# A hybrid encoder layer: TensorE's projection matmuls moved ahead of the turn in each attention unit

## The chip, the cores and the metric

The kernel runs on one core of a Trainium2 chip. The metric is device time in microseconds (us), the median of several runs. TensorE (PE in the profile, with its weight loads as PEld) does the matmuls and transposes, VectorE is DVE, ScalarE is ACT, GpSimd is POOL, and SyncE (SP) starts most DMAs.

## The reference

One layer on 1024 tokens of 1024 features: a half-step feed-forward block, a mixing block, a second half-step feed-forward block, each with a modulated layer norm ahead and a layer norm behind. The change lies in the mixing block:

```python
def _mixer(u, w_in, rpb, w_out):
    proj = u @ w_in                      # [qA kA vA | qB kB vB]
    ...
    ya = _dilated_attention(heads_a(qa), heads_a(ka), heads_a(va))
    yb = _neighbourhood_attention(heads_b(qb), heads_b(kb), heads_b(vb), rpb)
    return jnp.concatenate([ya, yb], axis=-1) @ w_out
```

Group A has 8 heads of 64 features with dilated windows, group B 8 heads with a two-dimensional neighbourhood of keys and a learned bias. Each is a softmax of masked scores times values.

## The kernel before, in words

The program runs phase after phase: modulation, feed-forward 1, a boundary phase, attention A, attention B, output projection, feed-forward 2. `attention_phase` is called twice, as phase A (tiles named `a_...`) and phase B (`b_...`).

A phase handles four pairs of heads. A pair has 16 units (`NU`): 8 blocks of 128 queries times 2 heads. So a phase has 64 units (`U`), and TensorE's program is one loop over s = 0 to 67. What a unit needs of each engine is handed on by semaphores:

- `score(s)`: TensorE computes the scores of unit s. In A that is a 128x256 product (L2082) and four 32-row products of 256 columns (L2085); in B one product of 128x384 (L2091). The program's fp32 matmul shows as two in the trace (so L2082 x2, L2085 x8, L2091 x2).
- `step(s)` on VectorE: waits for the scores, takes the reciprocal of unit s-2's row sums (L1962), adds the bias and takes the row minimum (L1967), then scales the exponentials of unit s-2 into `pn` (L1974).
- `exponential(s)` on ScalarE (L1876), behind L1967.
- `turn(s - LAG)`, with `LAG = 3`: TensorE transposes the 128x512 (A, four pieces) or 128x384 (B, three pieces) of `pn` (L2101) into a PSUM bank of `a_tr` or `b_tr`. It waits for `pn` of unit s-3, which VectorE makes in `step(s - 1)`, and for its bank.
- `turned_out` on ScalarE: copies that bank to SBUF (L1884). It stands in ScalarE's program behind `exponential(s)`, and ahead of the copies of projection results (`take`) and of the rounding of the next weights (`split`, L1869).
- `project(p + 1, ...)`: in each unit of pairs 0 to 2, TensorE runs `SPREAD = 9` of the 144 matmuls (L2042, 128x512, fp32r) which give the next pair's keys, queries and values. Pair 3 has no next pair, so its 16 units have no projection.
- Every eighth unit from s = 11 on ends with `multiply` (L2127, weights times values).
- Five units of a pair in A and four in B (unit 4 of pairs 1 to 3 on) end with `values(p, g)`: three or four transposes of values (L2069) into a bank of the same two banks, which VectorE copies out (L1922).

Each of TensorE's steps starts with waits of its own, and the engine takes its instructions in the program's order. VectorE's copy L1922 of group g stands in its program behind `step`, `take` and `split` (L1914, which waits for ScalarE's L1869).

Of the kernel before, what the change touches and what calls it, by code (L numbers as in the profile page):

```python
# [31 lines left out]
HP = HEADS // 2  # L32
# [1562 lines left out]
def band_start(t):  # L1595

    return min(max(P * t - HD, 0), S - BAND)
# [43 lines left out]
def attention_phase(nc, top, tag, w_in, w_at, w_next, y_at, ut_hi, ut_lo, scratch, ident, bias_in, tab, y_t,  # L1641
# [21 lines left out]
    SPREAD = 9  # L1663
# [12 lines left out]
    def outputs(p):  # L1676

        return [(j, half) for j in ((2, 1, 0) if p == 0 else (1, 0, 2)) for half in range(HALVES)]

    def output_at(p, j, half):  # L1680
        return NPJ * p + outputs(p).index((j, half))
# [9 lines left out]
    def split_at(g, j):  # L1691

        return 3 * (g - 1) + ((2, 1, 0) if g == 1 else (1, 0, 2)).index(j) + 1

    def values_due(s):

        p, g = s // NU, s % NU - LAG - 1
        return (p, g) if 1 <= p < HP and 0 <= g < NVG else None

    def half_due(s):  # L1700

        h = (s - LAG) // UN - 1
        return h if s >= LAG and (s - LAG) % UN == 0 and 0 <= h < 2 * HP else None
# [16 lines left out]
    with ExitStack() as st:  # L1720
# [302 lines left out]
        def _(pe):  # L2023
            def wait_taken(n):
                pe.wait_ge(pj_v, taken(n, True))
                if taken(n, False):
                    pe.wait_ge(pj_s, taken(n, False))

            def project(p, first, last):

                for x in range(first, last):
                    i, y_ = x // FULL, x % FULL
                    j, half = outputs(p)[i]
                    n = NPJ * p + i
                    if y_ == 0:
                        if p >= 1:
                            pe.wait_ge(w_lo, split_at(p, j))
                        if n >= 2:
                            wait_taken(n - 2)
                    k, m = y_ // 3, y_ % 3  # L2040
                    l, r = ((wh, ut_hi), (wh, ut_lo), (wl, ut_hi))[m]
                    done = nc.tensor.matmul(pj[:, half, :], l[:, k, j, :], r[:, k, NB * half:NB * half + NB],  # L2042
                                            start=y_ == 0, stop=y_ == FULL - 1, skip_group_check=True)
                    if y_ == FULL - 1:
                        done.then_inc(pj_mm, 1)
# [17 lines left out]
            def values(p, g):  # L2063
                if g == 0:
                    wait_taken(output_at(p, 2, 1))
                bank_free(("v", p, g))
                for x in range(VB * g, min(VB * g + VB, NV)):
                    at = P * (x - VB * g)
                    last = nc.tensor.transpose(tr[:, turn_at["v", p, g] % 2, at:at + P], value_source(x), ident[:, :])  # L2069
                last.then_inc(v_tr, 1)  # L2070

            def score(u):
                p, m, b = u // NU, u % NU, u % 2
                t, i = m // 2, m % 2
                if m == 0:
                    wait_taken(output_at(p, 0, 1))
                if u >= 2:
                    pe.wait_ge(low, u - 1)
                own = q[:, p % 2, i, :]
                if dil:  # L2080
                    w0 = band_start(t)
                    nc.tensor.matmul(sc[:, b, 0:BAND], own[:, P * t:P * t + P], keys[:, p % 2, w0:w0 + BAND],  # L2082
                                     start=True, stop=True, skip_group_check=True)
                    for r in range(CL):
                        last = nc.tensor.matmul(sc[CQ * r:CQ * r + CQ, b, BAND:BAND + CK],  # L2085
                                                own[:, P * t + CQ * r:P * t + CQ * r + CQ], kc[:, p % 2, r, :],
                                                start=True, stop=True, skip_group_check=True)
                else:
                    cb, rb = t // RBS, t % RBS
                    grid = keys[:, p % 2, :].rearrange("p (r c) -> p r c", c=COLS)  # L2090
                    last = nc.tensor.matmul(sc[:, b, 0:W], own[:, P * t:P * t + P],  # L2091
                                            grid[:, 4 * rb:4 * rb + KR, KC0[cb]:KC0[cb] + KC],
                                            start=True, stop=True)
                last.then_inc(qk, 1)

            def turn(u):
                b = u % 2
                pe.wait_ge(divided, u + 1)
                bank_free(("t", u))
                for c in range(NC):  # L2100
                    last = nc.tensor.transpose(tr[:, turn_at["t", u] % 2, P * c:P * c + P], pn[:, b, P * c:P * c + P],  # L2101
                                               ident[:, :])
                last.then_inc(p_tr, 1)

            def multiply(h):
                p, half = h // HALVES, h % HALVES
                pe.wait_ge(p_out, UN * (h + 1))
                if half == 0:
                    pe.wait_ge(v_out, NVG * (p + 1))
                if p >= 1:  # L2110
                    pe.wait_ge(y_out, HALVES * (p - 1) + half + 1)
                todo = products(dil, half)
                for n, (x, users, cls) in enumerate(todo):
                    for i in range(2):
                        to = o[HD * i:HD * i + HD, half, :]
                        if cls is not None:
                            to = to.rearrange("p (t r m) -> p t r m", r=CL, m=CQ)[:, :, cls]
                            of = pt[:, i, :, users[0][1], CQ * cls:CQ * cls + CQ]
                        else:
                            t, ch = users[0]  # L2120
                            to = to[:, P * t:P * (t + len(users))]
                            of = pt[:, i, t, ch]
                            if len(users) == 2:
                                at, step = (t * NC + ch) * P, (NC - 1) * P
                                of = pt_flat[:, i, at:at + 2 * step].rearrange(
                                    "p (a s) -> p a s", s=step)[:, :, 0:P]
                        last = nc.tensor.matmul(to, vt[:, x, HD * i:HD * i + HD], of, start=(n == 0),  # L2127
                                                stop=(n == len(todo) - 1), skip_group_check=True)
                last.then_inc(pv, 1)
# [8 lines left out]
            for s in range(U + LAG + 1):  # L2138
                p, m = s // NU, s % NU
                if s < U:  # L2140
                    score(s)
                if LAG <= s < U + LAG:
                    turn(s - LAG)
                if p + 1 < HP:
                    project(p + 1, SPREAD * m, SPREAD * m + SPREAD)
                if half_due(s) is not None:
                    multiply(half_due(s))
                if values_due(s):
                    values(*values_due(s))
# [213 lines left out]
```

## Time and profile before

| | before |
|---|---|
| median of 3 runs | 2155.69 us (2155.47 to 2156.41) |
| profiled execution | 2155.39 us, of which the span is 2153.5 us |
| PE / PEld / DVE / ACT / POOL busy | 91% / 71% / 56% / 37% / 32% |
| phase A, units 3 to 47 (turn and projection) | 858.5 to 1048.4 us |
| phase B, units 3 to 47 | 1152.15 to 1308.1 us |

The busy shares are averages over the whole layer. The stretches in the last two rows are the ones in which a unit has both a turn and projection matmuls. The time per unit is read there as the distance between the starts of two scores.

### The profile page before, as it was taken

The numbers are of one execution on the slowest core, as the hardware profiler recorded it, in microseconds if no ns is written. First come the engines' busy times: TensorE is split into PE (matmuls) and PEld (weight loads), VectorE is DVE, ScalarE is ACT, GpSimd is POOL, SyncE is SP. The second block draws the span as 40 slices with busy tenths as digits, with TensorE's granted clock in tenths as the row PEclk, the third lists the DMA queues.
The fourth block names the chain that finished last, engine by engine and source line by source line (L and its number), as shares of the span: only waits on it lengthen the run. The fifth ranks groups of instructions, "written<-read, shape, count | busy, mean of one in ns | idle before, by whom it ended". The sixth has DMA issues, their size and how long they took to land. (4 is left out here: it accounts for less than half of the span.)

```text
span 2153.5 us, 27570 instructions
## 1 busy us (share of the span) xinstructions
PE 1970.2 (91%) x10086; PEld 1536.9 (71%) x10086; DVE 1205.6 (56%) x2047; ACT 792.2 (37%) x1367; POOL 696.5 (32%) x488
## 2 busy tenths in 40 slices
PE   3999999999999938999889998894999999999996
PEld 2777777777878726677567775673888888888884
DVE  4865555545687973344423445467744444457778
ACT  2623333332434242433423344315433333334441
POOL 0653334332960020000023222232734343339400
PEclk6999999999999969999999999897999999999998
DMA  6255545454874133011032220603233332357732
GB/s 255 93 159 179 166 148 184 153 168 149 317 246 151 45 108 97 21 49 49 11 81 59 49 59 11 223 22 117 93 103 118 98 105 92 102 191 287 259 108 98
DMA packets 184663, 270.58 MB, mean 126 GB/s; under 512 B 12353, under 2 KB 110929, under 8 KB 184401
## 3 DMA queue, kind: packets, MB, share of 16 engines
q1 hardware_dynamic: 153410, 234.45, 32.3%
q10 hardware_dynamic: 30096, 30.25, 4.5%
q0 software_dynamic: 1024, 4.13, 1.2%
q8 instruction: 81, 1.33, 0.3%
q14 instruction: 52, 0.43, 0.1%
HBM read 210.85 MB, written 57.93 MB: 125 GB/s over the span
## 5 line engine op out<-in xcount | busy, mean ns | idle before, releaser
L1474 PE MATMUL f_ps<-f_uh,f_ops 128*128 128x512 f32 x2496 | 787.2, 392 | 5.9 <-DVE f_ops L1232 4.2
L1474 PEld LDWEIGHTS f_ps<-f_uh,f_ops 128*128 128x128 f32 x2496 | 468.7, 188 | 128.1 <-issue 25.3
L1474 PE MATMUL f_ps<-f_ul,f_ops 128*128 128x512 f32 x1248 | 486.0, 389 | 0.0
L1474 PEld LDWEIGHTS f_ps<-f_ul,f_ops 128*128 128x128 f32 x1248 | 234.5, 188 | 46.8
L1333 DVE TENSOR_TENSOR f_dl<-f_blocks,f_dh 128x1024 fp32r<-128x1024 f32 (+1 forms) x146 | 200.1, 1384 | 86.3 <-ACT f_dh L1158 86.0
L1158 ACT CAST f_dh<-f_blocks 128x1024 fp32r<-128x1024 f32 (+1 forms) x146 | 144.4, 990 | 229.0 <-PE f_ps L1581 222.9
L1581 PE MATMUL f_ps<-f_dh 128*128 128x512 f32 x496 | 195.9, 395 | 9.9 <-DVE f_ev L1367 5.3
L1232 DVE TENSOR_TENSOR f_ops<-f_sums,f_ops 128x512 fp32r<-128x512 f32 x160 | 122.4, 765 | 142.9 <-ACT f_ops L1045 142.9
L984 POOL TENSOR_TENSOR f_sums<-f_raw 128x512 f32<-128x512 f32 x80 | 107.4, 1342 | 280.2 <-DVE f_ops L1232 210.3
L1581 PE MATMUL f_ps<-f_dl,f_dh 128*128 128x512 f32 x496 | 194.9, 393 | 0.0
L1581 PE MATMUL f_ps<-f_dh,f_dl 128*128 128x512 f32 x496 | 194.8, 393 | 0.0
L1232 DVE TENSOR_TENSOR f_ops<-f_raw,f_ops 128x512 fp32r<-128x512 f32 x136 | 107.0, 789 | 112.3 <-ACT f_ops L1045 112.2
L2042 PE MATMUL in_pj<-ut_hi,in_wh 128*128 128x512 f32 x376 | 158.8, 422 | 9.2 <-PEq L2327 4.7
L1272 DVE TENSOR_TENSOR acc<-acc,f_ps 128x512 f32<-128x512 f32 x120 | 82.5, 687 | 139.2 <-PE f_ps L1474 139.0
L2042 PE MATMUL in_pj<-ut_hi,in_wl 128*128 128x512 f32 x376 | 149.3, 397 | 0.0
L2042 PE MATMUL in_pj<-ut_lo,in_wh 128*128 128x512 f32 x376 | 148.1, 394 | 0.0
L1581 PEld LDWEIGHTS f_ps<-f_dh 128*128 128x128 f32 x496 | 94.2, 190 | 33.8 <-DVE f_dl L1333 14.5
L1045 ACT CAST f_ops<-f_sums 128x512 fp32r<-128x512 f32 x160 | 95.5, 618 | 37.7 <-PE f_ps L1474 16.4
L1581 PEld LDWEIGHTS f_ps<-f_dh,f_dl 128*128 128x128 f32 x496 | 94.3, 190 | 19.9
L1581 PEld LDWEIGHTS f_ps<-f_dl,f_dh 128*128 128x128 f32 x496 | 94.1, 190 | 19.2
L1834 POOL MEMSET b_q<- 64x1024 f32 x4 | 3.7, 945 | 287.6 <-POOLq L2327 287.5
L1860 POOL TENSOR_TENSOR b_bias<-b_runs,b_mask 128x384 f32<-128x384 f32 x48 | 49.2, 1057 | 134.9 <-DVE b_sm L1967 112.5
(233 smaller groups left out, 3146.0 us busy)
## 6 DMA issues: line engine op xcount, KB each, us to landing
f_hidden<-acc SPq DMA_DIRECT2D x154, 256.0 KB, 3.8
f_blocks<-f_hidden SPq DMA_DIRECT2D x154, 256.0 KB, 3.4
f_blocks<-in_ffn_w_down SPq DMA_DIRECT2D x132, 256.0 KB, 5.8
f_raw<-in_ffn_w_gate SPq DMA_DIRECT2D x22, 1024.0 KB, 6.2
f_raw<-in_ffn_w_up SPq DMA_DIRECT2D x22, 1024.0 KB, 5.4
f_aw<-in_w_ada ACTq DMA_DIRECT2D x28, 512.0 KB, 3.5
acc<-in_w_ada ACTq DMA_DIRECT2D x28, 512.0 KB, 3.7
in_raw<-in_w_in SPq DMA_DIRECT2D x24, 512.0 KB, 4.0
```

What stands on the lines that cost most here:

```text
L984: nc.gpsimd.tensor_tensor(sums[:, x], of, with_, how).then_inc(s_done, 1)
L1045: nc.scalar.copy(op(o)[0], source(o)).then_inc(w_hi, 1)
L1158: nc.scalar.copy(high_of(n), operands(n)).then_inc(d_hi, 1)
L1232: nc.vector.tensor_tensor(op(o)[1], source(o), op(o)[0].bitcast(F32), ALU.subtract).then_inc(w_lo, 1)
L1272: nc.vector.tensor_tensor(to, t_in, ps[:, bank, :], ALU.add).then_inc(done, 1)
L1333: nc.vector.tensor_tensor(low_of(n), operands(n), high_of(n).bitcast(F32), ALU.subtract).then_inc(d_lo, 1)
L1474: done = nc.tensor.matmul(ps[:, bank, :], l[:, k, :], r[:, k, :], start=fresh and k == 0 and m == 0, stop=closed and k == HK - 1 and m == ...
L1581: done = nc.tensor.matmul(ps[:, bank(r, t), :], left[m][:, x, P * t:P * t + P], right[m], start=r in OPENS and k == 0 and m == 0, stop=r i ...
L1834: nc.gpsimd.memset(q[HD * (1 - i):HD * (2 - i), par, i, :], 0.0).then_inc(zeroed, 1)
L1860: nc.gpsimd.tensor_tensor(b, run, m, ALU.add).then_inc(b_ready, 1)
L2042: done = nc.tensor.matmul(pj[:, half, :], l[:, k, j, :], r[:, k, NB * half:NB * half + NB], start=y_ == 0, stop=y_ == FULL - 1, skip_group ...
```

## The change

In TensorE's loop, `project` now stands directly behind `score`, and `turn` behind `project`. Nothing is added or removed, no other engine's program differs, and no DMA is moved.

```diff
                 if s < U:
                     score(s)
+                if p + 1 < HP:
+                    project(p + 1, SPREAD * m, SPREAD * m + SPREAD)
                 if LAG <= s < U + LAG:
                     turn(s - LAG)
-                if p + 1 < HP:
-                    project(p + 1, SPREAD * m, SPREAD * m + SPREAD)
                 if half_due(s) is not None:
                     multiply(half_due(s))
                 if values_due(s):
```

On TensorE's queue in phase A this is one unit of pair 0, with a turn and neither `multiply` nor `values`. `a_sc` is the scores' PSUM tile, `in_pj` the projection's, and a row of the order is one matmul of the program.

```order
 L2082 MATMUL a_sc<-a_k,a_q 128x256
 L2085 MATMUL a_sc<-a_kc,a_q 32x256 x4
+L2042 MATMUL in_pj<-ut_hi,in_wh 128x512
+L2042 MATMUL in_pj<-ut_lo,in_wh 128x512
+L2042 MATMUL in_pj<-ut_hi,in_wl 128x512
...
 L2101 MATMUL a_tr<-ident,a_pn 128x128 x4
-L2042 MATMUL in_pj<-ut_hi,in_wh 128x512
-L2042 MATMUL in_pj<-ut_lo,in_wh 128x512
-L2042 MATMUL in_pj<-ut_hi,in_wl 128x512
...
```

The four transposes L2101 stood between the scores and the nine projection matmuls, and now stand between the ninth of these and the next unit's scores.

On TensorE's queue in phase A these are the rows around a unit that also has a group of value transposes (`a_tr<-ident,a_v`).

```order
+L2042 MATMUL in_pj<-ut_hi,in_wl 128x512
 L2101 MATMUL a_tr<-ident,a_pn 128x128 x4
-L2042 MATMUL in_pj<-ut_hi,in_wh 128x512
-L2042 MATMUL in_pj<-ut_lo,in_wh 128x512
-L2042 MATMUL in_pj<-ut_hi,in_wl 128x512
...
 L2069 MATMUL a_tr<-ident,a_v 128x128 x4
 L2082 MATMUL a_sc<-a_k,a_q 128x256
 L2085 MATMUL a_sc<-a_kc,a_q 32x256 x4
```

Here the turn now stands directly ahead of the value transposes, where nine matmuls lay between them; both still stand behind this unit's scores and ahead of the next unit's.

## Rows read from the trace of the kernel before

**Rows 1.** The page: span of the profiled execution.

```profile
span 2153.5 us, 27570 instructions
```

**Rows 2.** Busy time by stretch: start:end, length, PE, PEld, DVE, ACT, POOL, PEclk, DMA, GB/s.

```profile
858.50:1048.40 189.90, 189.17 (x1355) 133.40 (x1355) 81.14 (x218) 74.60 (x158) 0.00 (x0) 1.00 0.12 36
1048.40:1098.00 49.60, 39.37 (x382) 24.17 (x382) 25.32 (x76) 23.68 (x54) 0.00 (x0) 1.00 0.03 12
1152.15:1308.10 155.95, 155.54 (x824) 118.41 (x823) 68.50 (x235) 62.42 (x158) 41.88 (x50) 1.00 0.20 45
```

**Rows 3.** Waits of PE, 858.5 to 1048.4: total us, times, longest.

```profile
PE a_tr L2069 <- DVE acc L1922: 0.7, 2, 0.4
```

**Rows 4.** Waits of PE, 1152.1 to 1308.1.

```profile
PE b_tr L2069 <- DVE acc L1922: 0.4, 1, 0.4
```

**Rows 5.** Timeline, PE, phase A: two units without a turn, then one.

```profile
852.01 0.59 PE L2082 MATMUL a_sc<-a_k,a_q 128*128 128x256 f32 x2
...
853.10 0.50 PE L2042 MATMUL in_pj<-ut_hi,in_wh 128*128 128x512 f32 x1
...
858.54 0.59 PE L2082 MATMUL a_sc<-a_k,a_q 128*128 128x256 f32 x2
...
859.64 0.66 PE L2101 MATMUL a_tr<-ident,a_pn 128*128 128x128 f32 x4
```

**Rows 6.** Timeline, PE, phase A: scores five units apart, with turns.

```profile
902.71 0.59 PE L2082 MATMUL a_sc<-a_k,a_q 128*128 128x256 f32 x2
...
921.04 0.59 PE L2082 MATMUL a_sc<-a_k,a_q 128*128 128x256 f32 x2
```

**Rows 7.** Timeline, PE, phase A: value transposes behind projection, first and fourth group.

```profile
931.98 0.39 PE L2042 MATMUL in_pj<-ut_hi,in_wl 128*128 128x512 f32 x1
932.21 0.60 PE L2069 MATMUL a_tr<-ident,a_v 128*128 128x128 f32 x4
932.65 0.60 PE L2082 MATMUL a_sc<-a_k,a_q 128*128 128x256 f32 x2
...
944.30 0.39 PE L2042 MATMUL in_pj<-ut_hi,in_wl 128*128 128x512 f32 x1
945.05 0.75 PE L2069 MATMUL a_tr<-ident,a_v 128*128 128x128 f32 x4 [0.37 <-DVE acc L1922]
```

**Rows 8.** Timeline, PE, last pair of A: a turn between two scores.

```profile
1052.67 0.66 PE L2101 MATMUL a_tr<-ident,a_pn 128*128 128x128 f32 x4
1053.17 0.60 PE L2082 MATMUL a_sc<-a_k,a_q 128*128 128x256 f32 x2
```

**Rows 9.** Timeline, PE, phase B: scores around two units without and three with turns.

```profile
1146.70 0.81 PE L2091 MATMUL b_sc<-b_k,b_q 128*128 128x384 f32 x2
...
1152.15 0.81 PE L2091 MATMUL b_sc<-b_k,b_q 128*128 128x384 f32 x2
...
1161.27 0.81 PE L2091 MATMUL b_sc<-b_k,b_q 128*128 128x384 f32 x2
```

**Rows 10.** Timeline, PE, phase B: scores of one later unit and the next.

```profile
1200.78 0.81 PE L2091 MATMUL b_sc<-b_k,b_q 128*128 128x384 f32 x2
...
1203.83 0.81 PE L2091 MATMUL b_sc<-b_k,b_q 128*128 128x384 f32 x2
```

**Rows 11.** Timeline, all engines, phase A: around the fourth group of value transposes.

```profile
939.97 0.56 ACT L1884 COPY acc<-a_tr 128x512 f32<-128x512 f32 x1
...
940.42 0.61 PE L2069 MATMUL a_tr<-ident,a_v 128*128 128x128 f32 x4
...
941.38 1.06 ACT L1869 CAST in_wh<-in_raw 128x1024 fp32r<-128x1024 f32 x1
...
943.17 1.22 DVE L1914 TENSOR_TENSOR in_wl<-in_raw,in_wh 128x1024 fp32r<-128x1024 f32 x1
```

**Rows 12.** Timeline, PEld, phase A: weight loads of a turn and of value transposes.

```profile
900.13 0.42 PEld L2101 LDWEIGHTS a_tr<-ident,a_pn 128*128 128x128 f32 x4 [0.41 <-issue]
...
931.99 0.59 PEld L2069 LDWEIGHTS a_tr<-ident,a_v 128*128 128x128 f32 x4
```

## The prediction

> **What bounds the kernel now.** I first looked at the busy time by stretch, to see whose time a unit takes. In phase A, from unit 3 to unit 47, TensorE is busy for 189.17 of 189.90 us, VectorE for 81, ScalarE for 75; in phase B it is busy for 155.54 of 155.95 us [rows 2]. So in the units where the order changes, TensorE sets the time, at its full granted clock (1.00), and nobody else comes near. The last pair of A is another matter: no projection, TensorE busy for 39.37 of 49.60 us [rows 2]. There the order of instructions stays as it was.
>
> Then the waits of TensorE in these stretches: 0.7 us in A over two places and 0.4 us in B at one [rows 3, 4], all of them value transposes waiting for VectorE's copy out of their bank. The turn never waits here. That is the number that matters most: the obvious hope of the change is that projection work covers a turn that waits for `pn`. There is no such wait to cover. The turn of unit s-3 needs `pn` from `step(s - 1)`, which needs only the scores of the unit before; at its old place it was in time, and at its new place it comes a whole projection later.
>
> So all that is left is what TensorE itself pays for the changed neighbours, and what the later turn does to ScalarE. I read the first from starts in the timeline, since the busy durations overlap.
>
> **The change, part by part.**
>
> *A unit of A without a turn* is scores, then nine projection matmuls, then the next scores. This is just what the changed unit begins with. Two such units take 858.54 - 852.01 = 6.53 us, 3.265 each [rows 5]. The adjacency scores to projection is therefore measured in this trace.
>
> *A unit of A with a turn, old order*: (921.04 - 902.71)/5 = 3.666 us [rows 6]. The turn between scores and projection costs 3.666 - 3.265 = 0.401 us.
>
> *The turn at its new place*, behind projection and ahead of scores. The nearest row is the group of four value transposes, which stands exactly there, with the same shape and number: it starts 0.23 us after the last projection matmul (as any next matmul does) and the scores start 932.65 - 932.21 = 0.44 us later [rows 7]. So the new unit is 3.265 + 0.44 = 3.705 us, 0.04 more than before. The far row on one side is a turn between two scores in the last pair: 1053.17 - 1052.67 = 0.50 us [rows 8], 0.10 more than now. On the other side I see no reason why the turn should cost less than its present 0.40, so zero. I take the value transposes, since they have the same left and right neighbour; the last pair's turn has scores on its left.
>
> Why the difference? The trace shows the turn's first weight load starting only with its first matmul, 0.41 us after PEld's previous work, while the value transposes' first load, at 931.99, precedes its matmul at 932.21 [rows 7, 12]. Behind the scores somebody has to make that start uncovered: now the turn, afterwards the first projection matmul, which the 3.265 already contains. The Trainium skill, "TensorE: Matmul & The Clock Gate", section "Architectural detail: the array is 16x 32x32, not 1x 128x128", says that TensorE can pull weight loads ahead of matmuls in flight. Taken alone that speaks against any effect: loads hide at either place and the sum is 0. The rows agree with it behind projection and not behind A's 32-row scores.
>
> *How many.* 45 units in A (s = 3 to 47). In two of them the value transposes wait for VectorE: their start comes 945.05 - 944.30 = 0.75 us behind the last projection matmul, where 0.23 is normal [rows 7]. VectorE's time there counts from the scores, so 0.04 us vanish in that wait of 0.52. The five units that end with `multiply`, and those with value transposes, I count like the rest. 43 x 0.038 = 1.6 us.
>
> *Phase B.* Unit without a turn: (1152.15 - 1146.70)/2 = 2.725 us; with a turn (1161.27 - 1152.15)/3 = 3.04 [rows 9], and 1203.83 - 1200.78 = 3.05 further on [rows 10]. Three transposes behind projection are three quarters of 0.44, 0.33 us. New unit 3.055, so 0.005 to 0.015 more; 0.01 x 44 = 0.4 us. The gap is smaller since B's scores are full 128-row products.
>
> *ScalarE.* It takes its program in order, and the copy L1884 behind the turn now comes one projection later: that delays everything behind it (copies of projection results, the rounding L1869 of the next weights), and VectorE's L1914 waits for L1869, ahead of the very copy for which the value transposes wait. At that place, in the old order, the copy ran at 939.97 and L1869 at 941.38, with VectorE starting L1914 at 943.17 [rows 11]. In the new order the turn's transposes end where the value transposes begin now, 940.42 plus 0.04; its result is out some 0.2 us after, so the copy starts near 940.7, 0.7 us late. L1869 then runs from 942.1 and ends near 943.15. VectorE wants it at 943.17. The cover is used to the last hundredth; I take +0.1 us for the three places together (two in A, one in B), and up to 0.7 at each, 2.1 us, as the upper end. Elsewhere ScalarE is idle for over half of the stretch (75 of 190 us [rows 2]) and projection results are needed more than a unit after they are taken. The last pair starts with one copy pending, which fits ahead of its first exponential; I take 0. VectorE, GpSimd, SyncE and their DMAs keep their order, and no transfer is near its deadline here (DMA share 0.12 and 0.20 [rows 2]).
>
> **Sum.** 1.6 + 0.4 + 0.1 = +2.1 us. The span of 2153.5 us [rows 1] becomes 2155.6, the profiled execution's 2155.39 us 2157.5. That execution lies 0.3 us under the median of 2155.69, so a median would be near 2157.8; I give 2157.7. This is 0.1% slower, under the 0.2% (4.3 us) that a measurement of this kernel tells from no change.
>
> **The rivals.**
> - *The place makes no difference* (chance 0.20): the turn costs its 0.40 us anywhere, as by the pull-ahead of weight loads. For it: the B rows already differ by no more than their own spread, 3.04 against 3.05. Against: 0.44 read at the new place, in A. 2155.7 us.
> - *Slower: the turn pays its full price at the new place* (0.10). It has a wait for `pn` and one for its bank; if these keep its weight loads back even behind projection, it costs what it costs in the last pair, 0.50 us in A (+0.098 x 43 = 4.2 us), and in B the same 0.06 over three transposes, 0.39 (3.115 against 3.045: 0.07 x 44 = 3.1). Total +7.3: 2163.0 us. It counts as slower once a unit takes 0.05 us more on average. Against: value transposes also wait on semaphores there, and show 0.44.
> - *ScalarE hands the weights over late* (0.10): the three value waits grow by 0.7 each, 2.1 us in place of 0.1: 2159.8 us. For it: the missing slack above. Against: the arithmetic says just in time.
> - *Faster* (0.05): the three value waits go, 3 x 0.52 = 1.6 us, and the turn is not dearer: 2154.1 us. I see no mechanism, since VectorE's copy is not any earlier.
>
> My forecast itself, +1.2 to +2.8 us, has 0.55.
>
> **How the numbers follow.** The range leaves out the second and fourth rival and takes in the others with the spread of a median: 2154.9 to 2160.8 us. Faster by over 0.2% would need more than all waits of TensorE in both stretches: 0.03. Slower by over 0.2%: the second rival and a little of the third, 0.13. Within 0.2%: 0.84.
>
> **What would show it.** In the new trace: scores 3.70 to 3.71 us apart in plain units of A, 3.05 to 3.06 in B; from the turn's start to the next scores 0.44 in A and 0.33 in B; the first weight load of a turn ahead of its matmul; the copy L1884 at the start of the next unit; the three value waits at 0.5 to 0.6 us; the last pair of A still some 49.6 us. The prediction is wrong if turns start to wait for `pn` or a bank, if projection waits for its weights or its bank, or if the last pair changes by more than 1 us because ScalarE enters it late.

## The result and the profile after

The changed kernel takes 2159.24 us (median of 20 runs) where the kernel before takes 2155.83 us (median of 20 runs beside them). The ratio is 1.0017, 95% interval 1.0010 to 1.0024: 3.4 us slower by the medians, between 2.2 and 5.2 by the interval. The profiled execution took 2158.84 us, with a span of 2157.0 us.

The same two stretches, unit 3 to unit 47 of each phase, read as busy time by stretch (columns as in [rows 2]):

```profile
856.78:1048.65 191.87, 191.24 (x1354) 134.59 (x1353) 81.26 (x218) 77.79 (x157) 0.00 (x0) 1.00 0.11 36
1152.93:1308.94 156.01, 155.60 (x823) 119.52 (x822) 68.19 (x235) 65.41 (x157) 41.74 (x50) 1.00 0.19 45
```

Before, the same distances between scores were 1048.40 - 858.54 = 189.86 us in phase A and 1308.10 - 1152.15 = 155.95 us in phase B [rows 2, 5, 9]. So A grew by 2.0 us and B by 0.1 us. TensorE idles for 0.6 us in the stretch of A, where it idled for 0.7: the loss is no stall. It is in the distances of starts. The PE timeline of a plain unit of A:

```profile
897.72 0.60 PE L2082 MATMUL a_sc<-a_k,a_q 128*128 128x256 f32 x2
898.24 0.64 PE L2085 MATMUL a_sc<-a_kc,a_q 128*32 128x256 f32 x8
898.81 0.50 PE L2042 MATMUL in_pj<-ut_hi,in_wh 128*128 128x512 f32 x1
899.15 0.39 PE L2042 MATMUL in_pj<-ut_lo,in_wh 128*128 128x512 f32 x1
...
900.99 0.60 PE L2101 MATMUL a_tr<-ident,a_pn 128*128 128x128 f32 x4
901.43 0.60 PE L2082 MATMUL a_sc<-a_k,a_q 128*128 128x256 f32 x2
```

Read the first column. The turn now takes 901.43 - 900.99 = 0.44 us. The first projection matmul, behind the 32-row products, takes 899.15 - 898.81 = 0.34 us to the next start, where 0.23 is usual between projection matmuls. The unit takes 3.71 us against 3.666 [rows 6].

The turn's weights are now loaded ahead, starting 0.22 us before the matmuls (PEld timeline of the changed kernel; compare [rows 12]):

```profile
900.77 0.59 PEld L2101 LDWEIGHTS a_tr<-ident,a_pn 128*128 128x128 f32 x4
```

TensorE's waits in the stretch of A, against [rows 3]:

```profile
PE a_tr L2069 <- DVE acc L1922: 0.6, 2, 0.3
```

No turn waits, as none did before. In B it is one wait of 0.4 us, as in [rows 4]. And the place where ScalarE's delay could have hurt, all engines, against [rows 11]:

```profile
939.73 0.59 ACT L1884 COPY acc<-a_tr 128x512 f32<-128x512 f32 x1 [0.61 <-PE a_tr L2101]
...
939.98 0.60 PE L2082 MATMUL a_sc<-a_k,a_q 128*128 128x256 f32 x2
...
941.17 1.07 ACT L1869 CAST in_wh<-in_raw 128x1024 fp32r<-128x1024 f32 x1
...
942.28 1.22 DVE L1914 TENSOR_TENSOR in_wl<-in_raw,in_wh 128x1024 fp32r<-128x1024 f32 x1
```

ScalarE's rounding L1869 ends at 942.24 and VectorE's L1914 starts at 942.28, directly behind its own L1974. Before, L1869 ended at 942.44, 0.73 us ahead of L1914 [rows 11]. The later copy used up all this slack and cost nothing.

### The profile page after: what moved, and what is told of

Same layout as the page of the kernel before. It is cut to its first block and busy times, and to the rows that moved or that the text cites. A ratio compares the mean times of both kernels' runs of the same rounds, so it can differ in the third digit from the quotient of the medians.

```text
span 2157.0 us, 27570 instructions
## 1 busy us (share of the span) xinstructions
PE 1973.9 (92%) x10086; PEld 1540.4 (71%) x10086; DVE 1210.4 (56%) x2047; ACT 799.5 (37%) x1367; POOL 694.8 (32%) x488
## 5 line engine op out<-in xcount | busy, mean ns | idle before, releaser
L1333 DVE TENSOR_TENSOR f_dl<-f_blocks,f_dh 128x1024 fp32r<-128x1024 f32 (+1 forms) x146 | 204.7, 1413 | 83.7 <-ACT f_dh L1158 83.4
L2042 PE MATMUL in_pj<-ut_hi,in_wh 128*128 128x512 f32 x376 | 169.2, 450 | 9.2 <-PEq L2327 4.8
L2042 PEld LDWEIGHTS in_pj<-ut_hi,in_wh 128*128 128x128 f32 x376 | 71.8, 191 | 47.7 <-issue 29.4
```

Of the source, the lines that this page charges most:

```text
L1333: nc.vector.tensor_tensor(low_of(n), operands(n), high_of(n).bitcast(F32), ALU.subtract).then_inc(d_lo, 1)
```

## The experiments

Ratios are to the kernel before, run on the same chip. Their intervals are some 0.1% wide on either side (2 us), too wide to tell 2 us from 1 or 3. The stretches are far sharper. So each row gives both, and the verdict on a mechanism rests on the stretch. The stretches run from the scores of unit 3 to those of unit 48.

| kernel | ratio (95% interval) | A, us | B, us |
|---|---|---|---|
| before, again (e0_control) | 1.0001 (0.9992 to 1.0010) | 189.86 | 155.94 |
| changed | 1.0017 (1.0010 to 1.0024) | 191.87 | 156.01 |
| changed, again (e12_after_again) | 1.0018 (1.0010 to 1.0027) | 191.91 | 156.05 |
| A alone (e1_a_only) | 1.0010 (1.0001 to 1.0019) | 191.88 | 155.93 |
| B alone (e2_b_only) | 0.9994 (0.9985 to 1.0003) | 189.90 | 155.95 |
| turn behind the first projection matmul (e3_after_first) | 1.0016 (1.0007 to 1.0025) | 191.80 | 156.26 |
| one transpose in front, the rest behind (e4_split_turn) | 0.9995 (0.9986 to 1.0004) | 190.02 | 156.16 |
| 128-row scores last, old order (e8_wide_last_old) | 1.0012 (1.0003 to 1.0021) | 191.47 | 155.94 |
| 128-row scores last, new order (e9_wide_last_new) | 1.0016 (1.0007 to 1.0025) | 191.36 | 155.95 |
| values copied out first, old order (e7_values_first) | 0.9989 (0.9981 to 0.9998) | 188.45 | 155.29 |
| values copied out first, new order (e11_values_first_new) | 0.9994 (0.9986 to 1.0003) | 190.54 | 155.43 |
| LAG = 2, old order (e5_lag2_old) | 1.0698 (1.0680 to 1.0715) | 249.18 | 212.57 |
| LAG = 2, new order (e6_lag2_new) | 1.0143 (1.0128 to 1.0158) | 191.81 | 155.56 |

### The control, and each phase by itself

The control is the kernel before with no edit.

> The kernel before once more, unchanged, as a control. Of the 3.4 us measured for the change, the trace shows 2.0 us in the stretch with turn and projection of phase A and 0.1 us in that of phase B; the other 1.3 us lie in the other phases. Theory O (order alone, the rest is the spread of the other phases): ratio 1.000 within 0.001, and the phases before and behind attention differ from those of the first trace by 1 us or more all the same. Theory E (the change also lengthens other phases): the other phases of this run agree with the first trace within some tenths.

The stretches come back within 0.02 us. The rest of the span doesn't quite: 2153.8 - 189.86 - 155.94 = 1808.0 us in the control, and 2157.0 - 191.87 - 156.01 = 1809.1 us in the changed kernel. That is a difference of 1.1 us between different kernels; the control and the first profile of before agree to 0.3 us there, which leans to theory E. The repeat of the changed kernel, below, decides about it.

For one phase alone, the loop has `turn` on both sides of `project`, each with a condition:

```diff
-                if LAG <= s < U + LAG:
+                if LAG <= s < U + LAG and not dil:
                     turn(s - LAG)
                 if p + 1 < HP:
                     project(p + 1, SPREAD * m, SPREAD * m + SPREAD)
+                if LAG <= s < U + LAG and dil:
+                    turn(s - LAG)
```

That is A alone; B alone has the two conditions exchanged.

> The turn moved behind the projection in phase A alone. Theory O: the stretch from unit 3 to 47 of A is 2.0 us longer (191.9 in place of 189.9), B as before; time +2.0 us. Rival E: A alone gives only part of it, some +1.5 us, since B or the phases behind contribute the rest.

> The turn moved behind the projection in phase B alone. Theory O: the stretch of B changes by 0.1 us (0 to +0.4), time within 0.5 us of before. Rival E: +1 us or more although the stretch of B has not become longer.

A alone lengthens its stretch by 2.0 us and shows +0.10%, 2.2 us. B alone leaves its stretch as it was, and its interval reaches only to +0.03%. So the loss is phase A's, and B contributes nothing to speak of.

How far the whole time of A alone goes back to its stretch is less sure, for the profile shows a second thing. From the scores of unit 48 to those of unit 63, in the last pair of A, the changed kernel and A alone run the same instructions in the same order. Busy time there, first in the changed kernel, then in A alone (the eighth number is the mean granted clock):

```profile
1048.65:1091.70 43.05, 35.02 (x344) 21.32 (x342) 22.29 (x66) 19.22 (x43) 0.00 (x0) 1.00 0.03 13
1048.20:1092.59 44.39, 36.34 (x343) 22.29 (x342) 22.30 (x66) 19.20 (x43) 0.00 (x0) 0.96 0.03 13
```

In this pair TensorE is idle for 8 us, and in A alone its granted clock was 0.50 (1.2 GHz) from 1056.5 to 1059.9 us: the pair took 1.3 us longer. The profiles of e3, e7, e8, e9 and e11 show the same mean of 0.96 in this pair; both profiles of before, both of the changed kernel, B alone, e4, e5 and e6 show 1.00. Each of these other kernels was profiled once, so whether all their executions have the drop isn't shown. It lies outside the two stretches, but their ratios may contain it.

### What the neighbours cost

The turn is put behind the first of the nine projection matmuls, in both phases.

```diff
                 if p + 1 < HP:
-                    project(p + 1, SPREAD * m, SPREAD * m + SPREAD)
+                    project(p + 1, SPREAD * m, SPREAD * m + 1)
+                if LAG <= s < U + LAG:
+                    turn(s - LAG)
+                if p + 1 < HP:
+                    project(p + 1, SPREAD * m + 1, SPREAD * m + SPREAD)
```

> Both phases: the turn stands behind the first projection matmul of the unit, eight follow. Theory L (whatever stands behind A's four 32-row score products starts with an uncovered weight load, and the projection matmul pays 0.11 us for that start where the turn pays 0.06): a plain unit of A takes 3.71 us as in the changed kernel, time +2 us. Rival R (the turn costs more ahead of the next scores): a unit of A takes 3.67 us as before, time +0.

The PE timeline of one unit of A:

```profile
862.81 0.64 PE L2085 MATMUL a_sc<-a_kc,a_q 128*32 128x256 f32 x8
863.38 0.50 PE L2042 MATMUL in_pj<-ut_hi,in_wh 128*128 128x512 f32 x1
863.72 0.60 PE L2101 MATMUL a_tr<-ident,a_pn 128*128 128x128 f32 x4
864.07 0.48 PE L2042 MATMUL in_pj<-ut_lo,in_wh 128*128 128x512 f32 x1
864.39 0.39 PE L2042 MATMUL in_pj<-ut_hi,in_wl 128*128 128x512 f32 x1
```

The turn is nowhere near the next scores, and the stretch is 191.80 us all the same. Rival R (the turn costs more ahead of the next scores) gave 3.67 us a unit and the old stretch here, and falls. What this order shares with the changed one is the projection matmul directly behind the 32-row products, with its 0.34 us.

The 0.32 us behind the turn here (864.39 - 864.07) is not a second such price. Behind a turn the first projection matmul's recorded start comes early, and its distance to the next is longer by as much. So the turn has to be read up to the second projection matmul behind it: 864.39 - 863.72 = 0.67 us here, just four transposes at 0.11 and one matmul at 0.23. In the kernel before, where the turn stands behind the 32-row products, the same distance is 942.69 - 941.96 = 0.73 us, 0.06 more (PE timeline):

```profile
941.96 0.66 PE L2101 MATMUL a_tr<-ident,a_pn 128*128 128x128 f32 x4
942.37 0.47 PE L2042 MATMUL in_pj<-ut_hi,in_wh 128*128 128x512 f32 x1
942.69 0.39 PE L2042 MATMUL in_pj<-ut_lo,in_wh 128*128 128x512 f32 x1
```

The complement: one transpose stays behind the scores, the others go behind the projection (`pieces` says which of the turn's transposes are issued; the waits stay with the first, the signal with the last).

```diff
                 if LAG <= s < U + LAG:
-                    turn(s - LAG)
+                    turn(s - LAG, [0])
                 if p + 1 < HP:
                     project(p + 1, SPREAD * m, SPREAD * m + SPREAD)
+                if LAG <= s < U + LAG:
+                    turn(s - LAG, range(1, NC))
```

> Both phases: the first transpose of the turn stays directly behind the scores, the other three (two in B) stand behind the ninth projection matmul. Theory L: the first transpose takes the uncovered start, so a plain unit of A takes 3.67 us as before although three quarters of the turn are at the new place; time within 0.5 us of before. Rival R: three quarters of the loss, 3.70 us a unit, +1.5 us.

```profile
862.10 0.60 PE L2082 MATMUL a_sc<-a_k,a_q 128*128 128x256 f32 x2
862.62 0.64 PE L2085 MATMUL a_sc<-a_kc,a_q 128*32 128x256 f32 x8
863.19 0.33 PE L2102 MATMUL a_tr<-ident,a_pn 128*128 128x128 f32 x1
863.28 0.48 PE L2042 MATMUL in_pj<-ut_hi,in_wh 128*128 128x512 f32 x1
...
865.44 0.49 PE L2102 MATMUL a_tr<-ident,a_pn 128*128 128x128 f32 x3
865.77 0.60 PE L2082 MATMUL a_sc<-a_k,a_q 128*128 128x256 f32 x2
```

3.67 us a unit (865.77 - 862.10). Three of four transposes stand at the new place, and all but 0.2 of the 2.0 us is gone. So what matters in A is which instruction follows the 32-row products.

Last, the neighbour itself is changed: in A's scores the 32-row products come first and the 128-row product last (the signal moves to the last), with either order of turn and projection.

```diff
-                    nc.tensor.matmul(sc[:, b, 0:BAND], own[:, P * t:P * t + P], keys[:, p % 2, w0:w0 + BAND],
-                                     start=True, stop=True, skip_group_check=True)
                     for r in range(CL):
-                        last = nc.tensor.matmul(sc[CQ * r:CQ * r + CQ, b, BAND:BAND + CK],
+                        nc.tensor.matmul(sc[CQ * r:CQ * r + CQ, b, BAND:BAND + CK],
...
+                    last = nc.tensor.matmul(sc[:, b, 0:BAND], own[:, P * t:P * t + P], keys[:, p % 2, w0:w0 + BAND],
+                                            start=True, stop=True, skip_group_check=True)
```

> Order of before, but in A's scores the four 32-row products come first and the 128-row product last, so that the turn follows a 128-row product. Theory L: the turn's start is covered, its first interval 0.109 in place of 0.166 us, 0.06 us less per unit, 64 units: -3 to -4 us at most, less what the projection-to-32-row change costs (0 to 0.09 us per unit, which would eat it). Rival R: nothing changes but that cost.

> The changed kernel with the 128-row product last in A's scores. Theory L: now the first projection matmul is covered too, so the difference between the two orders goes: a plain unit of A takes the same as in the kernel with this edit and the old order, within 0.01 us. Rival R: the new order still costs 0.04 us per unit more.

In the old order:

```profile
863.12 0.40 PE L2042 MATMUL in_pj<-ut_hi,in_wl 128*128 128x512 f32 x1
863.44 0.64 PE L2083 MATMUL a_sc<-a_kc,a_q 128*32 128x256 f32 x8
864.01 0.70 PE L2086 MATMUL a_sc<-a_k,a_q 128*128 128x256 f32 x2
864.55 0.60 PE L2101 MATMUL a_tr<-ident,a_pn 128*128 128x128 f32 x4
864.90 0.47 PE L2042 MATMUL in_pj<-ut_hi,in_wh 128*128 128x512 f32 x1
865.22 0.39 PE L2042 MATMUL in_pj<-ut_lo,in_wh 128*128 128x512 f32 x1
```

The turn, read up to the second projection matmul, now takes 0.67 us in place of 0.73, since its start is covered; but the way into the 32-row products costs 0.32 us where 0.23 is usual. Net this edit is a loss, 191.47 against 189.86 us. In the new order:

```profile
864.18 0.70 PE L2086 MATMUL a_sc<-a_k,a_q 128*128 128x256 f32 x2
864.53 0.58 PE L2042 MATMUL in_pj<-ut_hi,in_wh 128*128 128x512 f32 x1
864.95 0.39 PE L2042 MATMUL in_pj<-ut_lo,in_wh 128*128 128x512 f32 x1
```

Here 864.95 - 864.18 = 0.77 us is the usual 0.54 of the 128-row product (864.55 - 864.01 above) and 0.23 of a projection matmul: this matmul pays nothing behind a 128-row product. The point is the comparison of the two kernels: 191.36 us with the new order, 191.47 with the old. With no 32-row product ahead of them, turn and projection can change places for nothing. I had expected the edit to gain up to 4 us in the old order if the way in were free; it isn't.

### Where the same move would be worth 114 us

With `LAG = 2` the turn of unit s-2 needs `pn` from the step of the same unit.

```diff
-    LAG = 3
+    LAG = 2
```

> Order of before, but the turn runs two units behind the scores in place of three (LAG = 2), in both phases. Now the turn of unit s-2 needs pn from VectorE's step of the same unit s, which starts only when the scores of s are done: in the trace of before pn is ready 1.3 us after the turn's place. Every theory: TensorE waits for pn in each of the 90 units, some 1.3 us each, about +110 us, plus a longer last pair.

> The changed order with LAG = 2. Theory L (the changed order buys 2.1 us of cover for the turn's wait, and there was no wait to cover): the nine projection matmuls (2.1 us) cover the 1.3 us, so the stretches with projection take about what they take in the changed kernel (191.9 and 156.0 us), and only the last pairs are longer. So the same move is worth some 100 us here, against -3 us with LAG = 3. Rival: the stall moves to the next scores or to a bank and most of the 110 us stays.

TensorE's waits in the stretch of A, old order:

```profile
PE a_tr L2101 <- DVE a_pn L1974: 57.7, 45, 1.3
```

and with the new order:

```profile
PE a_tr L2069 <- DVE acc L1922: 0.6, 2, 0.3
```

45 waits of 1.3 us are gone; the stretches fall from 249.18 + 212.57 to 191.81 + 155.56 us, 114 us, and the medians from 2308.7 to 2187.7 us. (Both are slower than the kernel before also in the last pairs, which have no projection to cover anything.) So moving the projection does what it looks like. With `LAG = 3` the lag had already bought that cover.

### The wait that was there

VectorE's copy of the value transposes moves directly behind `step`, ahead of `take` and `split`:

```diff
                 if s < U + 2:
                     step(s)
+                if values_due(s - 1):
+                    values(*values_due(s - 1))
                 for g, i in ended_in(s - 1):
                     take(g, i, dve)
...
-                if values_due(s - 1):
-                    values(*values_due(s - 1))
```

> Order of before; VectorE copies the value transposes out directly behind its step, ahead of the projection copies and of the weights' low part. The three waits of TensorE for that copy (two in A, one in B, 0.5 us each by distance of starts) should go: -1.6 us, and some of the 4.4 us that the last pair of A waits for the same copy may go too. Rival: the waits only move, 0.

Both stretches lose their waits: TensorE is busy in every instant of them.

```profile
859.80:1048.25 188.45, 188.45 (x1354) 133.69 (x1353) 81.07 (x218) 74.54 (x158) 0.00 (x0) 1.00 0.12 36
```

1.4 us less in A and 0.65 in B; the ratio is 0.9989 (0.9981 to 0.9998), some 2.4 us faster than before. The hope for the last pair did not come true: TensorE still waits 4.4 us there for the same copy, and in this profile the drop of the clock makes its 15 units 1.6 us longer (44.61 against 43.05). From unit 3 of A to unit 48 of B the profile is thus only 0.4 us shorter than before (449.2 against 449.6). The ratio is the lowest of the study, but the intervals of B alone, e4 and e11 overlap with it.

> The changed order together with VectorE's copy of the value transposes ahead of its other copies. Theory O: the two edits are independent: stretches 191.9 - 1.4 + 0.04 x 2 = 190.5 us and 156.0 - 0.6 = 155.4 us, time about as before (+0.1 us). Rival: in the new order ScalarE hands the weights over late and the gain of the copy order is lost, +1 us or more.

With the new order A takes 190.54 us: 191.87 less 1.4, and 2.1 us more than with the old order. The two edits add up in the stretches, and ScalarE's delay costs nothing here either.

### Once more the changed kernel

> The changed kernel once more, unchanged. First time it was 3.4 us slower by the runs, while the two stretches with turn and projection grew by 2.1 us. Theory O (only the stretches grow, the rest is spread): the stretches are again 191.9 and 156.0 us, and the ratio lies nearer to 1.0010 (+2.1 us) than to 1.0017. Rival E (1.3 us more in other phases is real): ratio again 1.0016 or more.

Neither theory comes out whole. The ratio repeats, 1.0018, as rival E said. But in this profile the rest of the span is 2152.9 - 191.91 - 156.05 = 1804.9 us, 3 us less than in the control. The rest of the span differs by 4 us between two profiles of one kernel, so one pair of profiles can't place the missing 1.3 us. One part of it does show in both: from the scores of A's unit 48 to those of B's unit 3 the kernel before takes 103.75 and 103.67 us, the changed one 104.28 and 104.30. The last pair of A is no part of this, with 43.04 to 43.06 us in all four profiles. Behind the pause between the phases, B's first projection starts at half the clock. The PE timelines of the kernel before and of the changed one show how long:

```profile
1109.16 0.63 PE L2042 MATMUL in_pj<-ut_hi,in_wl 128*128 128x512 f32 x1
1109.59 0.58 PE L2042 MATMUL in_pj<-ut_hi,in_wh 128*128 128x512 f32 x1
1110.00 0.39 PE L2042 MATMUL in_pj<-ut_lo,in_wh 128*128 128x512 f32 x1
```

```profile
1110.70 0.63 PE L2042 MATMUL in_pj<-ut_hi,in_wl 128*128 128x512 f32 x1
1111.13 0.52 PE L2042 MATMUL in_pj<-ut_hi,in_wh 128*128 128x512 f32 x1
1111.48 0.39 PE L2042 MATMUL in_pj<-ut_lo,in_wh 128*128 128x512 f32 x1
```

The matmuls start 0.43 us apart at 1.2 GHz and 0.23 us apart at 2.4 GHz. The first of this row of matmuls started at 1105.61 before and at 1105.87 after, so full speed returned 4.4 us behind it before and 5.6 us after, three matmuls later. Busy time in 24.5 us from just ahead of that start, before and after:

```profile
1105.50:1130.00 24.50, 24.39 (x101) 20.02 (x102) 3.34 (x6) 2.40 (x6) 14.65 (x19) 0.91 0.64 155
```

```profile
1105.80:1130.30 24.50, 24.43 (x96) 19.98 (x97) 3.34 (x6) 2.14 (x5) 14.72 (x20) 0.89 0.64 155
```

In the first, TensorE gets through the 96 projection matmuls of this place and five transposes behind them, at a mean granted clock of 0.91; in the second through the 96 alone, at 0.89. Both profiles of the kernel before show 101, both of the changed kernel 96, and A alone 101. Three matmuls at 0.2 us more each are 0.6 us. Why the clock should return later there I didn't test. The order in A doesn't do it by itself, for A alone had full speed back after 4.4 us. In the other kernels it took 3.7 to 5.2 us, so what is lost here varies from program to program by more than 0.6 us.

With it the profiles place 2.0 + 0.1 + 0.6 = 2.7 us. The other 0.7 us is not located, and it need not exist: both intervals of the changed kernel begin at 1.0010, 2.2 us.

## Why the prediction was right

*TensorE sets the time in these units, and no turn waits*: right before and after. With `LAG = 2` the turn does wait, 1.3 us a unit, and there the same move pays.

*The price of the move, 1.6 us in A*: right in mechanism and a little small, with 2.0 us measured in the stretch. The value transposes were the right row to read: 0.44 us for the turn. The unit came out at 3.71 and not 3.705, and from unit 29 on even at 3.74 in places. Most of that last step is projection matmuls that start a few nanoseconds further apart. Why they do is open. Unit 31:

```profile
975.00 0.60 PE L2082 MATMUL a_sc<-a_k,a_q 128*128 128x256 f32 x2
...
978.74 0.60 PE L2082 MATMUL a_sc<-a_k,a_q 128*128 128x256 f32 x2
```

*The reason, that somebody must make an uncovered start behind A's 32-row products*: shown, by e3, e4, e8 and e9. The account is sharper now. Counted at its own place, the turn looks 0.04 us dearer. In truth its 0.44 us are four transposes at 0.11 with nothing on top. The uncovered start moved to the projection matmul, which pays 0.34 - 0.23 = 0.11 us for it, while the turn had paid 0.73 - 0.67 = 0.06. The difference is the 0.05 us a unit that the stretch shows (2.0 us over 43 units). The last pair's 0.50 us [rows 8], which the prediction could only put down to another neighbour on the left, is the same 0.44 + 0.06. The Trainium skill's rule that TensorE can pull weight loads ahead of matmuls in flight ("TensorE: Matmul & The Clock Gate", "Architectural detail: the array is 16x 32x32, not 1x 128x128") holds behind 128-row matmuls in this trace (900.77 ahead of 900.99) and not behind the 32-row ones (PEld idle for 0.41 us up to the turn's first load [rows 12]), and so does not make the order free.

*B, 0.4 us*: measured 0.1. The term was too large: it multiplied a difference of 0.01 us, no larger than the spread of its rows, by 44.

*ScalarE just in time, 0.1 us*: right to 0.04 us at the place read; the rival with 2.1 us fell, and the three waits didn't grow.

*The sum, +2.1 us*: 2.0 + 0.1 in the profiled stretches. By the runs the change costs 3.4 us (2.2 to 5.2), 1.3 more. That is above the forecast's own +1.2 to +2.8 us, though the interval reaches into it; the median of 2159.24 us lies in the stated range because the range also takes in the rivals and a spread. It even lies nearer to the 2159.8 us of the rival that ScalarE hands the weights over late, which did not happen. So the direction and the mechanism came true, and the total was met less well than the stretches. The sum had no term for the clock at the head of phase B, 0.6 us; the rest is open. The other rivals: the free order falls in A and holds in B; the full price of 0.50 us fell, as the turn's weights are loaded ahead at its new place; nothing made it faster.

## What to carry to other kernels

Moving work ahead of a waiting instruction helps only where that instruction waits: read its wait first. Where there is none, an order still has a price of tens of nanoseconds per place, set by what stands next to what; look in the trace for the same pair of neighbours (first iterations and side branches often have them) and multiply. And a stretch in which TensorE hardly pauses can be compared to 0.04 us between profiles (189.86 and 189.86, 191.87 and 191.91), where the whole kernel spreads over several us. Look at its granted clock first: the last pair of A, with its waits, took 1.3 to 1.7 us more in the profiles of e1, e3, e7 and e11, where the clock had dropped.

## What was unexpected of the hardware

Changing to or from products of 32 rows of output has a price in both directions: from projection into them 0.32 us where 0.23 is usual (e8), and out of them 0.06 us more for a transpose (the kernel before) and 0.11 us more for a 512-column fp32r matmul (the changed kernel).

The time until the clock is back at 2.4 GHz after the pause between the phases was 4.4 us in the kernel before and 5.6 us in the changed one, with the same work there, and was the same within 0.1 us in both profiles of each.

A short drop of the clock in the last pair of A came in six of the fourteen profiles: A alone had it (a mean of 0.96), and the changed kernel, with the same order of instructions in A, did not (1.00 in both profiles).
